# Reordering the stretch between the last output-projection tile and the first expert

## What is computed

```
x  = x + gt1 * (merged @ w_o)
h2 = rmsnorm(x, g_ffn) * (1 + sc2) + sh2
logits = h2 @ w_router + b_router
top_val, top_idx = top_k(logits, 4);  gates = softmax(top_val)
# every expert e, for the tokens that chose it:
g, u = split(h2 @ w_gate_up[e] + b_gate_up[e]);  g = min(g, 7);  u = clip(u, -7, 7)
out  = ((u + 1) * g * sigmoid(1.702 * g)) @ w_down[e] + b_down[e]
x  = x + gt2 * sum over the four experts of gate * out
y  = rmsnorm(x, norm_final_g)
```

## Time and profile before

| | |
|---|---|
| median of 3 runs | 1404.57 us (1404.45 to 1405.47) |
| span of the profiled execution | 1402.6 us |
| PE busy in the span | 1364.6 us (97%) |
| PEld / DVE / ACT / POOL busy | 556.0 / 502.6 / 220.2 / 69.3 us |
| mean granted TensorE clock | 0.996 |
| DMA | 487.27 MB, mean 347 GB/s |
| chain that ended last | PE 57%, DMA 17%, DVE 1% |

### The profile page before, as it was taken

One profiled execution on the slowest core, in us unless ns is written; L12 is line 12 of the kernel. 1 busy time (PEld: TensorE's weight loads), 2 busy tenths in 40 slices (PEclk: granted clock), 3 DMA queues, 4 the chain that ended last, 5 costly groups with the idle time before them and its releaser, 6 DMA issues.

```text
span 1402.6 us, 17315 instructions
## 1 busy us (share of the span) xinstructions
PE 1364.6 (97%) x6624; PEld 556.0 (40%) x6624; DVE 502.6 (36%) x1075; ACT 220.2 (16%) x406; POOL 69.3 (5%) x64
## 2 busy tenths in 40 slices
PE   8999999999999999999999999999999999999996
PEld 3544555555456433333333333333333333333332
DVE  3135887853222432233223322332223222233224
ACT  2111232221011301011111110111111111111102
POOL 1103402220001000000000000000000000000000
PEclk9999999999999999999999999999999999999998
DMA  9524354387768699999999999999999999999994
GB/s 384 170 87 163 121 120 164 104 310 279 310 262 334 255 390 427 429 425 429 430 427 428 429 428 428 428 429 428 429 429 428 429 429 427 429 430 427 429 427 164
DMA packets 62013, 487.27 MB, mean 347 GB/s; under 512 B 8295, under 2 KB 30247, under 8 KB 33164
## 3 DMA queue, kind: packets, MB, share of 16 engines
q1 hardware_dynamic: 59660, 481.91, 83.5%
q0 software_dynamic: 1152, 4.19, 0.7%
q10 hardware_dynamic: 1152, 0.52, 0.1%
HBM read 482.49 MB, written 4.08 MB: 347 GB/s over the span
## 4 chain that ended last, share of the span: by engine, by line
PE 57%; DMA 17%; DVE 1%; issue 0%; ACT 0%; DVEq 0%; SPq 0%
PE ps L1721 23%; DMA ring<-in_w_gate_up 14%; PE ps L1748 13%; PE ps L1656 5%; PE ps L1693 4%; PE ps L1524 3%; DMA ring<-in_w_down 2%; PE ps L1707 2%; PE ps L1025 1%; PE ps L1026 1%; PE ps L1664 1%; PE ps L1734 1%; PE ps L1697 1%; PE ps L1359 1%; PE ps L1029 0%
## 5 line engine op out<-in xcount | busy, mean ns | idle before, releaser
L1721 PE MATMUL ps<-ring,z 128*64 128x512 f32 x1552 | 343.7, 594 | 9.7 <-DMA ring<-in_w_gate_up 9.0
L2414 DVE TENSOR_SCALAR actT<-ps 128x512 f32<-128x512 f32 x32 | 22.1, 692 | 589.0 <-PE ps L1721 589.0
L1721 PEld LDWEIGHTS ps<-ring,z 128*64 128x64 f32 x1552 | 108.5, 137 | 239.3 <-issue 217.6
L1748 PE MATMUL ps<-ring,z 128*64 128x512 f32 x752 | 167.7, 594 | 0.1
L1048 PE MATMUL ps<-ring,actT 128*128 128x512 f32 (+1 forms) x208 | 105.8, 590 | 0.0
L1049 PE MATMUL ps<-ring,actT 128*128 128x512 f32 (+1 forms) x208 | 103.7, 580 | 0.0
L1748 PEld LDWEIGHTS ps<-ring,z 128*64 128x64 f32 x752 | 52.5, 137 | 110.1 <-issue 109.1
L1656 PE MATMUL ps<-z,actT 128*64 128x512 f32 x384 | 89.1, 596 | 1.2 <-DVE actT L2330 1.2
L1693 PE MATMUL ps<-z,aT 128*128 128x512 f32 x120 | 62.0, 619 | 0.0
L2359 DVE TENSOR_TENSOR xr<-xr,z 128x512 f32<-128x512 f32 (+1 forms) x75 | 59.8, 797 | 2.6
L1721 PE MATMUL ps<-z 128*64 128x512 f32 x256 | 57.8, 593 | 2.8 <-DMA z<-in_w_gate_up 2.8
(11 more groups left out here) (372 smaller groups left out, 1330.3 us busy)
## 6 DMA issues: line engine op xcount, KB each, us to landing
ring<-in_w_gate_up SPq DMA_DIRECT2D x97, 2048.0 KB, 26.6
ring<-in_w_down SPq DMA_DIRECT2D x47, 2048.0 KB, 29.1
z<-in_w_gate_up SPq DMA_DIRECT2D x16, 2048.0 KB, 27.1
more_w<-in_w_gate_up SPq DMA_DIRECT2D x15, 2048.0 KB, 25.9
ring<-in_w_ada SPq DMA_DIRECT2D x11, 2048.0 KB, 10.8
ring<-in_w_in SPq DMA_DIRECT2D x11, 2048.0 KB, 7.9
more_w<-in_w_down SPq DMA_DIRECT2D x9, 2048.0 KB, 30.1
z<-in_w_down SPq DMA_DIRECT2D x8, 2048.0 KB, 32.7
```

What stands on the lines that cost most here:

```text
L1721: done = nc.tensor.matmul(bank(q // 2)[64 * (q % 2):64 * (q % 2) + 64, :], lhs, homes[home][4 * (k % 2) + q], start=False, stop=k == 7)
L1748: done = nc.tensor.matmul(bank(2)[64 * q:64 * q + 64, :], lhs, homes[home][2 * (k % 4) + q], start=k == 0, stop=k == 7)
```

## The change

On PE, router step 7 moves between the two sums of squares. All eight row products of `uc` for the samples move behind the positions (step 7 of the list), and the transposes of `x1c` for t = 0 move from there into expert 0, behind its `gate_up`. On ACT, the copy of `x3` for t = 0 moves from ahead of the experts to behind expert 0's sigmoid. On DVE, the four clears move ahead of the wait for `sq_sum`. The counts of `rows_tr` that are waited for follow the new order.

```diff
@@ scalar
             act.wait_ge(rstd2_done, 1)
-            act.wait_ge(rows_tr, 14)
+            act.wait_ge(rows_tr, 13)
             nc.scalar.activation(h2[:, 1, :], bank(6, 2), ACT.Copy, scale=st[:, 12:13]).then_inc(rows_done, 1)
...
-            x1_rows_out(0)
-
...
                 if sums and half == 0:
+                    x1_rows_out(0)
                     x1_rows_out(2)
@@ tensor
+            def square_sums(sq, first):
                 for t in range(3):
                     n = TOK[t]
                     last = nc.tensor.matmul(bank((0, 1, 6)[t])[0:n, 0:1], sq[:, t * P:t * P + n], const("ones")[:, 0:1],
-                                            start=sq is sqa, stop=sq is not sqa)
-            last.then_inc(sq_sum, 1)
+                                            start=first, stop=not first)
+                if not first:
+                    last.then_inc(sq_sum, 1)
+
+            router_steps(4, KT - 1)
+            pe.wait_ge(g2_done, 2)
+            pe.wait_ge(pool_sum, KT - 2)
+            pe.wait_ge(x1_done, KT - 1)
+            square_sums(sqa, True)
             router_steps(KT - 1, KT)
-            rows_of(uc, 2, 4, KT - 1)
+            pe.wait_ge(ss2_done, KT)
+            square_sums(sqc[KT - 1], False)
             router_rows()
...
             last.then_inc(pos_mm, 1)
-            pe.wait_ge(rows_done, 13)
-            rows_of(x1c, 0, 6)
+            rows_of(uc, 2, 4)
             pe.wait_ge(h2_done, 1)
...
                 if s == 0 and sums:
+                    pe.wait_ge(rows_done, 13)
+                    rows_of(x1c, 0, 6)
+                    pe.wait_ge(h2s_done, 1)
                     rows_of(x1c, 2, 4)
@@ vector
+            nc.vector.memset(m8r, 3.0e38)
+            nc.vector.memset(lrep, 0.0)
+            nc.vector.memset(sel_m, 0.0)
+            step(nc.vector.memset(gate_r, 0.0))
             dve.wait_ge(sq_sum, 2)
...
-            nc.vector.memset(m8r, 3.0e38)
-            nc.vector.memset(lrep, 0.0)
-            nc.vector.memset(sel_m, 0.0)
-            step(nc.vector.memset(gate_r, 0.0))
...
-            dve.wait_ge(rows_tr, 15)
+            dve.wait_ge(rows_tr, 14)
             nc.vector.scalar_tensor_tensor(h2[:, 0, :], bank(0, 2), st[:, 11:12], sh2p, ALU.mult, ALU.add).then_inc(h2_done, 1)
...
-            dve.wait_ge(rows_tr, 13)
+            dve.wait_ge(rows_tr, 15)
             dve.wait_ge(part_done, 6)
```

## The result

The changed kernel takes 1408.63 us in the median of 20 runs (1404.58 to 1410.2), the kernel before 1405.47 us on the same occasions (20 runs, 1403.16 to 1407.12): ratio 1.0017, 95% interval 1.001 to 1.0023. It is slower by 2.4 to 3.2 us, by ratio and by medians; forecast was +0.5, and 1408.63 is outside the range. Of the distance to the forecast time, 0.9 us is the kernel before itself, which had 1404.57 us in the three runs that the prediction started from; 1408.63 less 0.9 is still above 1406.4. The profiled execution has a span of 1404.6 us against 1402.6, +2.0.

What follows compares the result with a forecast made beforehand. The weight stream was taken to bound the kernel, its last dry place ended by the fifth release (chunk 12). -0.65 us in front + 1.15 in expert 0 = +0.5, so 1404.57 + 0.5 = 1405.1 us; range 1403.6 to 1406.4.

Steps and rivals of the forecast that it cites:

- What bounds the kernel: Whole kernel: the weight stream sets the end, which moves one to one with the fifth release, the one starting chunk 12.
- Part 1: Router step 7 to logits by rows: the new order starts the logits by rows 0.65 us earlier.
- its late neighbour: Behind the second sum of squares: PE idles 1.0 us, waiting for ACT's root and copy; no cost counted.
- part 2: Logits by rows to expert 0: distances stay, moved work is hidden, so expert 0's weights start 0.65 us earlier, at 467.28.
- rival C: Ahead of expert 0: late sample row products delay DVE's `h2` and the gather, +1.7 us in sum, 1406.3 us; chance 0.07.
- Part 3: Inside expert 0, behind `gate_up`: eight moved transposes and two width changes cost 1.15 us before the fifth release.
- The sum: At the fifth release: 0.65 us won in front, 1.15 us paid in expert 0, net +0.5 us.
- A: Rival, at the sums of squares: stationary width changes eat the front's gain, +1.0 us, 1405.5 us; chance 0.15.
- B: Rival, expert 0: first release counts or moved transposes are hidden, so the end moves by -0.65 us, 1403.9 us; chance 0.11.

Runs made afterwards that it cites:

- e3: Kernel before with only the transposes of `x1c` for t = 0 and ACT's copy of `x3` moved into expert 0: median +2.4 us against 1405.0, ratio 1.0017.
- f5: e4 with both sums of squares ahead of router step 7, three sample row products behind it and five behind the positions: ratio 0.9985 to the kernel before.
- f7: Kernel before with only DVE's four clears moved ahead of its wait for the sums: no difference, chunk 12 at +42.47 us as before.
- e1: Changed kernel with two unread 128x320 products filling PE's wait behind the second sum of squares: median within noise of the kernel before, chunk 12 0.57 us later.
- g1: Kernel before with two 128x512 products spread among the thin column products at 402 to 408 us: median 1402.72 us.
- g3: e1 with the early move of two 128x512 products as in g1: median 1402.83 us.
- e4: Changed kernel with four sample row products in PE's gap and the t = 0 transposes back ahead of the experts: median 0.9 us below the kernel before, interval includes 1.
- g2: Changed kernel with the early move of two 128x512 products as in g1: median 1404.27 us.

## Why the prediction was wrong

**What bounds the kernel: right.** The end followed chunk 12: +2.17 against a span of +2.0. The last expert's `gate_up` starts at 1351.35 us before and at 1353.51 after, 2.16 us later. Across all kernels the span less the time of chunk 12 is 907.7 to 909.8 us. The traces show where most of these 2 us arise. From chunk 12 to the last `gate_up` it is 856.7 to 857.2 us in ten kernels and 857.7 to 858.1 in e3, f5 and f7, which stays open. From the last half of `down` to the issue of the last output it is 18.95 to 18.97 us in ten, and 20.16 to 20.47 in e1, g1 and g3: there the clock fell once more, ahead of 1394 us, under the last six instructions of the products with 512 columns (4.54 instead of 3.03 us in g1). A single span is only as good as that.

**Part 1, the order: right; its late neighbour: the step that failed.** The gain at the logits by rows was 0.59 us, counted from the first router step, and 0.60 at the weights (e1); forecast 0.65. The failed sentence is "PE now idles there for 1.0 us (454.98 to 455.98); that is late next, with ACT's root and copy in front of it". The idle time was found to 0.1 us and taken as free. It costs the clock: with it, weights at +17.05; with the same order and the time filled, +15.40. So, counted from the first router step, 1.64 of the 2.21 us by which chunk 12 is late is that (+44.68 against +43.04 in e1), and the other 0.57 is the sum as forecast. The same blindness is in part 2, "The transposes of `x1c` that leave were in the shadow of DVE and POOL, so taking them away gains nothing there": they gained nothing and cost 1.6 us at the weights when they left alone (e3).

**Part 2, "They keep their distances, so all move by 0.65 us": wrong for that reason only.** In e1 they keep them. The clears were worth nothing, as said (f7). The sample row products were hidden at full clock (e1, e4); in the changed kernel they start at 462.30, with the clock just back, because what stands ahead of them ran at 1.2 GHz, and DVE waited 0.42 us for them ahead of 463.92: rival C, set off by the clock.

**Part 3: right.** From the weights' start to chunk 12: 496.57 - 468.94 = 27.63 against 26.47 us, +1.16; forecast +1.15. The eight transposes stand at 482.82 and issue in about 1.0 us.

**The sum** at an unbroken clock: +0.57 (e1), forecast +0.5. **Rivals.** A is out: variances at 455.02. B is out: the weights' start moved by 1.0 us, the end by 2.0; and over all thirteen kernels the span less the start of expert 0's weights is on average 1.3 us longer where the eight transposes stand in expert 0 (changed, e1, e3, g2, g3), while the span less chunk 12 differs by 0.2. What the prediction set against the change, the added width changes in the front, was counted wrongly: between router step 4 and the logits by rows the stationary width changes five times before (32, 64, 128, 32, 64, 128 columns) and three times after (32, 128, 32, 128). No rival had the clock, though its mean of 0.996 in the kernel before said that it falls somewhere, and the prediction itself listed an idle microsecond behind products with one column. A range that ended 0.1 us above the slowest priced rival (C, 1406.3) had no room for it.

**Median against profile.** +3.2 in the medians, +2.0 in the profile. Mean granted clocks of the changed kernel's 20 runs are 0.991 to 0.996 (17 of them below 0.995, which is the commonest value of the kernel before), and the profiled one, the third fastest of the 20, had 0.994: ten executions had 0.993 or less and so lost more than the one that is shown. Where they lost it, no trace here tells. With the early fall out of the way the change costs 1.55 us (g2 against g1), not 2.4 to 3.2; why the rest goes with it isn't known, since the early place is the same in both orders.

## What to carry to other kernels

When an edit takes PE's work out of a wait, the wait is not free even off the critical path: the next microseconds of PE may run at 1.2 GHz, as in the changed kernel and e3. A long row of narrow products (here of 9 columns, with transposes) can have the same effect without any wait. Put work that is owed anyway into the wait, as e4 and f5 do, and read the column PEclk in steps of 1 us before and after. In a kernel that ends on a stream of weights, price every edit at the release that ended the last dry place.

## What the hardware showed that I had not expected

The granted clock fell with PE busy without a break, amid products of 9 columns (e1, 405.0 us) or just behind 5 us of them and of transposes (kernel before, 407.8 us), and it fell in 1.08 us of idle time behind sums of one column (changed kernel). Stretches of 1 us have it at 1.00 or 0.50, or between the two where one holds a change. What a fall costs depends on what stands under it: 0.47 us in g1, 1.65 in the changed kernel, and at the early place up to 3.5 (the first router step is at 449.09 us in e4, without a fall there, and at 452.61 in e1, with 6.8 us of it). All thirteen profiles also have it at 0.50 in the last 18 us. Two dense products of 128x320 at the right place were enough to keep it up in both profiles that have them (e1, g3). No kernel was profiled in two executions, but the early place is the same code in nine of them and shows 0, 3.4 or 6.8 us. Such differences fit the spread of the runs, though that link isn't shown: of the 35 runs of the kernel before that went with e1 to e4, the seven with a mean clock of 0.996 had 1403.5 us on average, the six with 0.994 had 1405.8.
